# Expert rows sent to their tokens by indirect transfers through DRAM in place of scatter products, in three of four expert groups of one layer

## What is computed

```python
g_idx = top-1 of 4 groups;  e_idx = top-2 of that group's 4 experts
w = pg_top * pe_top / sum(pe_top)
expert = g_idx * 4 + e_idx
gates = sum(one_hot(expert, 16) * w[..., None], axis=1)
for e in range(16):
    he = silu(t @ w1[e]) * (t @ w3[e])        # 1024 -> 512
    out = out + gates[:, e:e + 1] * (he @ w2[e])   # 512 -> 1024
```

## Time and profile before

| | us |
|---|---|
| median of 3 runs | 892.6 (890.75 to 893.31) |
| the profiled execution | 893.93 |
| its span | 892.2 |
| TensorE busy | 830.9 (93%) |
| DVE, ACT, POOL busy | 317.2, 201.9, 151.8 |

### The profile page before, as it was taken

The page is one execution under the profiler, slowest core; times in us unless marked ns, Lnnn a source line. Parts: engine busy times, 40 slices in busy tenths (PEclk is TensorE's granted clock), DMA queues, the critical chain, the costliest instruction groups (busy, mean ns, idle before and its releaser), DMA issues.

```text
span 892.2 us, 12858 instructions
## 1 busy us (share of the span) xinstructions
PE 830.9 (93%) x5263; PEld 459.3 (51%) x5264; DVE 317.2 (36%) x720; ACT 201.9 (23%) x332; POOL 151.8 (17%) x242
## 2 busy tenths in 40 slices
PE   3899989899999999999499999699999899999994
PEld 1367644565465564655456554434444554655651
DVE  1437994551131321411799421621000311311304
ACT  2403330531221311312500110411001211312212
POOL 2418679039200000000133100100000000000000
PEclk9899999999999999999799999889999999999998
DMA  9999999949999999994996882206766299999972
GB/s 329 345 363 387 346 374 324 364 178 423 421 422 421 421 422 423 422 421 170 391 339 235 305 334 98 92 1 237 307 240 251 99 415 421 419 424 421 422 296 72
DMA packets 69185, 285.37 MB, mean 320 GB/s; under 512 B 7260, under 2 KB 8572, under 8 KB 44312
## 3 DMA queue, kind: packets, MB, share of 16 engines
q1 hardware_dynamic: 66208, 277.88, 79.8%
q0 software_dynamic: 2240, 5.24, 1.7%
q10 hardware_dynamic: 696, 1.68, 0.5%
HBM read 279.55 MB, written 5.24 MB: 319 GB/s over the span
## 4 chain that ended last, share of the span: by engine, by line
PE 85%; DVE 8%; DMA 3%; SPq 2%; ACT 1%; issue 1%; DVEq 0%; ACTq 0%
PE PS L1713 22%; PE PS L1732 14%; PE PS L1740 8%; PE PS L1756 7%; PE PS L2019 7%; PE PS L1716 6%; PE PS L1445 4%; PE PS L1671 3%; PE PS L1475 3%; DMA ring<-in_ab_w_in 2%; PE PS L1537 2%; PE PS L2004 2%; PE PS L1554 2%; SPq L379 2%; PE PS L1982 1%
## 5 line engine op out<-in xcount | busy, mean ns | idle before, releaser
L1732 PE MATMUL PS<-ring,work 128*64 128x512 f32 (+1 forms) x512 | 128.4, 595 | 0.0
L1713 PE MATMUL PS<-ring,hT 128*64 128x256 f32 x896 | 107.3, 381 | 0.0
L1713 PE MATMUL PS<-ring,yg 128*64 128x256 f32 x896 | 106.2, 379 | 0.0
L1320 DVE TENSOR_TENSOR work<-work,PS 128x512 f32<-128x512 f32 x32 | 22.0, 688 | 198.7 <-PE PS L1713 150.4
L1713 PEld LDWEIGHTS PS<-ring,hT 128*64 128x64 f32 x896 | 62.5, 137 | 40.5 <-issue 10.3
L1732 PEld LDWEIGHTS PS<-ring,work 128*64 128x64 f32 (+1 forms) x512 | 43.0, 143 | 74.3 <-issue 73.3
L1713 PEld LDWEIGHTS PS<-ring,yg 128*64 128x64 f32 x896 | 64.4, 137 | 32.3
L1740 PE MATMUL PS<-work,xhat 128*128 128x256 f32 (+1 forms) x256 | 68.2, 426 | 7.8 <-issue 7.4
L1324 DVE COPY yg<-PS 128x512 f32<-128x512 f32 x32 | 22.1, 692 | 144.8 <-PE PS L1732 144.8
L1756 PE MATMUL PS<-yg,grow 64*128 64x512 f32 (+1 forms) x256 | 68.0, 606 | 0.0
L1740 PEld LDWEIGHTS PS<-work,xhat 128*128 128x128 f32 x256 | 50.1, 198 | 28.5 <-issue 22.2
(11 more groups left out here) (379 smaller groups left out, 997.9 us busy)
## 6 DMA issues: line engine op xcount, KB each, us to landing
ring<-in_moe_w SPq DMA_DIRECT2D x96, 2048.0 KB, 13.6
ring<-in_ada_w SPq DMA_DIRECT2D x20, 2048.0 KB, 15.8
work<-in_ada_w SPq DMA_DIRECT2D x4, 2048.0 KB, 13.8
ring<-in_s_glu_w SPq DMA_DIRECT2D x4, 2048.0 KB, 17.1
ring<-in_ab_w_in SPq DMA_DIRECT2D x3, 2048.0 KB, 24.1
ring<-in_ab_w_out SPq DMA_DIRECT2D x2, 2048.0 KB, 13.4
ring<-rot_tables SPq DMA_DIRECT2D x2, 2048.0 KB, 10.9
rot_tables<-grow POOLq DMA_DIRECT2D x8, 256.0 KB, 5.6
```

The lines of the kernel that those rows point to most:

```text
L1320: v.tensor_tensor(pairs_out(he[:, e % 2, :]), pairs_out(he[:, e % 2, :]), pairs(bank[1]), ALU.mult).then_inc(S("he_ready"), 1)
L1713: last = mm(dst[64 * u:64 * u + 64, 0:256], hg[k][:, e * P:e * P + 64], w[:, k, 256 * u:256 * u + 256], start=k == 0, stop=k == KD - 1)
L1732: last = mm(dst, left[:, at:at + (64 if narrow else P)], w[:, c4, h * HALF:(h + 1) * HALF], start=c4 == 0, stop=c4 == KF - 1)
```

## The change

In layer 1, groups 0 to 2 (`DIRECT = 3`) no longer use `turn_weights` and `scatter`. A small product, `slot_info`, gives for each slot its destination row number and its gate weight. DVE's `rows_out` multiplies each expert's product by weight and `gfrow` while it takes it from PSUM into `yg`, and GpSimd's `spread` sends the two halves of these rows to the DRAM tensor `y_rows` by indirect transfers, with numbers out of range for unfilled slots. Rows of tokens that the three groups do not serve are cleared by `clear_rows`. SP reads `y_rows` back (`back`, 4 x 512 KB) between the sixth and the seventh weight unit of group 3, and DVE adds it to x in group 3 (`add_back`). With the banks free, hidden products alternate between two bank pairs and the transposes between banks 6 and 7. Group 3 keeps the scatter products and now opens `acc` itself. In both layers the gate arithmetic (`gates`) stands behind the picks. Several semaphores are merged (`table_dve`, `table_act`) without moving work.

```diff
+                if L == 1:
+                    sp_.wait_ge(S("spread_out"), 64 + 32 * EPG * DIRECT)
+                    for w in range(2):
+                        for b in range(NB):
+                            src = y_rows.rearrange("(b p w h) n -> b w p h n", b=NB, w=2, h=2)[b, w]
+                            sp_.dma_start(back[:, w, b, :].rearrange("p (h n) -> p h n", h=2), src).then_inc(
+                                S("rows_back"), 16)
                 for j in range(SLOTS, PER_GROUP):
                     free_slot(n0 + (NG - 1) * PER_GROUP + j)
                     send_expert(L, j, NG - 1)
...
+            def clear_rows():
+                pool.wait_ge(S("gates_ready"), 1)
...
+                ch.link(g.memset(zero_row, 0.0))
+                for b in range(NB):
+                    for w in range(2):
+                        g.indirect_dma_start(y_rows.rearrange("(t h) n -> t (h n)", h=2),
+                                             bass.IndirectOffsetOnAxis(ap=row_no[:, NG - 1, b, w:w + 1], axis=0), zero_row,
+                                             None, bounds_check=2 * T - 1, oob_is_err=False).then_inc(S("spread_out"), 16)
+                pool.wait_ge(S("spread_out"), 64)
+            def spread(i, e):
+                pool.wait_ge(S("y_dve"), PRIMED["y_dve"] + 16 + 4 * i + e + 1)
+                for h in range(2):
+                    g.indirect_dma_start(y_rows[:, :], bass.IndirectOffsetOnAxis(ap=row_no[:, i, e, h:h + 1], axis=0),
+                                         yg[:, e % 2, h * HALF:(h + 1) * HALF], None, bounds_check=4 * T - 1,
+                                         oob_is_err=False).then_inc(S("spread_out"), 16)
+                pool.wait_ge(S("spread_out"), 64 + 32 * (4 * i + e + 1))
+                pool.sem_inc(S("y_gone"), 1)
+
             over_row(1)
+            clear_rows()
+            for i in range(DIRECT):
+                for e in range(EPG):
+                    spread(i, e)
...
+                    def rows_out(e):
+                        dve.wait_ge(S("y_ps"), e0 + e + 1)
+                        dve.wait_ge(S("y_gone"), 1 + e0 - 16 + e)
+                        for h in range(2):
+                            part = slice(h * HALF, (h + 1) * HALF)
+                            last = v.scalar_tensor_tensor(yg[:, e % 2, part], bank[(6 if e == 3 else 4) + h], slot_w[:, e:e + 1],
+                                                          gfrow[:, part], ALU.mult, ALU.mult)
+                        last.then_inc(S("y_dve"), 1)
+                    def add_back(w):
+                        dve.wait_ge(S("rows_back"), 64)
+                        for b in range(NB):
+                            for h in range(2):
+                                part = slice(h * HALF, (h + 1) * HALF)
+                                last = v.tensor_tensor(x[:, b, part], x[:, b, part], back[:, w, b, part], ALU.add)
...
                 slots(krow[:, 0, :])
                 picks(krow[:, 0, :])
                 link(v.tensor_copy(kcur, krow[:, 0, :]))
+                gates()
...
+            def slot_info():
+                for e in range(EPG):
+                    for b in range(NB):
+                        last = mm(bank[7][:, 2 * e:2 * e + 2], pick[:, b, e, :], slot_in[:, b, e, :], start=b == 0,
+                                  stop=b == NB - 1)
+                return last
...
+                    def down_direct(e, narrow):
+                        j = AT[("w2", e)]
+                        loaded(pe, n0 + j, i)
+                        pe.wait_ge(S("heT_ready"), 1 + e0 + e + 1)
+                        if 1 <= e < 3:
+                            pe.wait_ge(S("y_dve"), 1 + e0 + e)
+                        product_down(u3(n0 + j, D), narrow, heTs[e % 2], 6 if e == 3 else 4,
+                                     (lambda: turned_direct(3, narrow)) if e == 2 else None).then_inc(S("y_ps"), 1)
...
                         gather(narrow)
+                        if direct:
+                            slots()
+                            for e in range(EPG):
+                                up(e, narrow)
+                                if e:
+                                    down_direct(e - 1, narrow)
+                            down_direct(EPG - 1, narrow)
+                            return
+                        if L == 1:
+                            for m in range(4):
+                                open_acc(m)
                         up(0, narrow)
```

More of the change, by code:

```diff
@@ L231, in build @@
         strips = pickW[:, :, :, :].rearrange("p b e n -> p (b e n)")[:, 0:T]
+        heTs = [heT, pickW[:, 0].rearrange("p e n -> p (e n)")]
+        first_row = rt[:, 316:318]
+        slot_in = rt[:, 80:96].rearrange("p (b e n) -> p b e n", b=NB, e=EPG)
+        slot_w = rt[:, 96:100]
+        below = before[:, 64:65]
+        miss, none, at_row = rt[:, 240:242], rt[:, 242:246], rt[:, 184:188]
+        y_rows = nc.dram_tensor("y_rows", [4 * T, HALF], F32).ap()
+        back = w3(T0, 2, NB, D)
         krow = rt[:, 248:248 + 9 * (NG + 1)].rearrange("p (g n) -> p g n", n=9)
@@ L461, in _ @@
             g = nc.gpsimd
+            pool.sem_inc(S("y_gone"), PRIMED["y_gone"])
             ch = Chain(pool, S("pool_order"))
@@ L834, in ffn, with group @@
                 pt = lambda m: pickT[:, 2 * m:2 * m + 2, :].rearrange("p e t -> p (e t)")
-                with act.Fori(0, NG) as i:
+                def group(i, direct):
                     gi, e0 = 4 * L + i, 16 * L + 4 * i
@@ L840, in silu, with he_direct @@
                         act.wait_ge(S("a_ps"), e0 + e + 1)
-                        s.activation(pairs_out(he[:, e % 2, :]), pairs(bank[0]), ACT.Silu).then_inc(S("sil_ready"), 1)
+                        s.activation(pairs_out(he[:, e % 2, :]), pairs(bank[e % 2 * 2 if direct else 0]), ACT.Silu).then_inc(
+                            S("sil_ready"), 1)
+                    def he_direct(e):
+                        act.wait_ge(S("heT_ps"), e0 + e + 1)
+                        s.activation(heTs[e % 2], bank[6 + e % 2], ACT.Copy).then_inc(S("heT_ready"), 1)
                     def he_t(e):
@@ L868, in ffn @@
                     y_out(3)
+                with act.Fori(0, NG if L == 0 else DIRECT) as i:
+                    group(i, L == 1)
+                if L == 1:
+                    group(NG - 1, False)
                 act.wait_ge(S("over_known"), L + 1)
@@ L1322, in y_out @@
+                    def add_back(w):
+                        dve.wait_ge(S("rows_back"), 64)
+                        for b in range(NB):
+                            for h in range(2):
+                                part = slice(h * HALF, (h + 1) * HALF)
+                                last = v.tensor_tensor(x[:, b, part], x[:, b, part], back[:, w, b, part], ALU.add)
+                        link(last)
                     def y_out(e):
@@ L1728, in product_down @@
                     steps = [(h, c4) for c4 in range(KF) for h in range(2)]
-                for h, c4 in steps:
+                for n_, (h, c4) in enumerate(steps):
+                    if halfway is not None and n_ == KF:
+                        halfway()
                     at = (c4 % 2) * P + (c4 // 2) * 64 if narrow else c4 * P
@@ L1889, in group, with wide_aside @@
                         spread(3, narrow)
+                    kind = f"{L}d" if direct else f"{L}"
                     is_narrow = pe.value_load(rti[0:1, bass.ds(i + 2, 1)], min_val=0, max_val=1)
                     head = nc.cur_bb
[L1893 to L1894 removed]
+                    nc.br_lt(is_narrow, 1, on_true=f"wide{kind}", on_false=f"narrow{kind}", engines=PE_ONLY)
+                    nc.switch_bb(f"narrow{kind}")
                     group(True)
[L1896 to L1897 removed]
+                    nc.br(f"group_end{kind}", engines=PE_ONLY)
+                    nc.switch_bb(f"group_end{kind}", parent=head)
+                    def wide_aside():
+                        with nc.body(f"wide{kind}", parent=head, valid_engines=PE_ONLY):
+                            group(False)
+                            nc.br(f"group_end{kind}", engines=PE_ONLY)
+                    return wide_aside
+                with pe.Fori(0, NG if L == 0 else DIRECT) as i:
+                    wides = [group_of(i, L == 1)]
+                if L == 1:
+                    wides.append(group_of(NG - 1, False))
                 for _ in range(SLOTS):
@@ L1937, in aside @@
                 def aside():
-                    with nc.body(f"wide{L}", parent=head, valid_engines=PE_ONLY):
-                        group(False)
-                        nc.br(f"group_end{L}", engines=PE_ONLY)
+                    for wide_aside in wides:
+                        wide_aside()
                     with nc.body(f"over{L}", parent=exit_, valid_engines=PE_ONLY):
```

235 lines of the change are left out of this document (167 added, 68 removed).

## The result

The changed kernel takes 878.09 us (median of 4 runs, 876.47 to 879.58), the kernel before 891.93 us in the same comparison. The ratio is 0.9841, 95% interval 0.9817 to 0.9866: 1.6% faster, by 12 to 16 us. The forecast was 12.7 us less, 879.9.

The account below looks back on a forecast made before the run. TensorE and the nearly equal, saturated weight stream bound it; the stream then decides. Last weights 851.6 + 5.0 + 2.6 = 859.2, then 3.5, 3.6 and 1.1: TensorE ends at 867.4 against 880.1; -12.7 from 892.6 gives 879.9 us, range 874 to 889.

Parts of the forecast that it names:

- Part 1: Gate arithmetic behind the picks, both layers: first gather 0.9 us earlier in layer 1, 0.4 us in layer 0.
- taking accumulator openers out of the routing stretch gives nothing: Layer 1's routing stretch: removing openers gains nothing, since TensorE waits for DVE there anyway.
- Part 2: Group 0, TensorE: weight transposes -0.9, scatter products -13.7, slot products +1.8, net -12.8 us.
- Part 3: Layer 1's weight stream starts when group 1's first weights are read, moving from 712.3 to 700.0 us.
- Parts 4 and 5: Groups 1 and 2: TensorE loses 6.7 us each, but the stream decides; read-back adds 4.97 us, scattered rows 2.6.
- Scatters: GpSimd's two transfers take 6 to 12 us an expert, hidden under 15 us (narrow group) or 25 (wide).
- the lock: SBUF: DVE operations in a two-port mode keep GpSimd from writing descriptors; no size given.
- Second rival: GpSimd's scatter sets the pace above 15.2 us an expert; gain gone at 16.8, 918 us at 20; chance 0.10.
- the rule's 15 us: Groups 1 and 2: eight experts each pay the excess of scatter time over 15.2 us.

Follow-up runs that it names:

- The fillers: Changed kernel with four filler products (full 512-column, into banks 4 to 7) where the openers stood in layer 1's routing stretch: 878.89 us, ratio 0.9825.

## Why the prediction was right, and where it was not

The mechanism was right. Group 0 gives its TensorE time in full, groups 1 and 2 give almost none, as the stream of weights takes over, and the read-back lengthens it. The run with one direct group shows the first two: with group 0 alone it is 9.8 us faster than the kernel before (893.35 to 883.55), and its group 0 takes 102.0 us from gather to gather (586.37 to 688.33). The runs without the read-back and with it last show the third.

- *Part 1.* Layer 0's gather comes 3.96 us after the last rank product instead of 4.53, so it gave 0.6 us, forecast 0.4. In layer 1 the step "taking accumulator openers out of the routing stretch gives nothing" was wrong: it costs 1.0 us through the clock, so that the part's 0.9 us came to nothing. The fillers show it, and the two later runs with fillers have 18.4 and 18.5 us.
- *Part 2.* Group 0 without the passage went from 115.1 to 101.8 us, -13.3; forecast -12.8. The slot products took 1.84 us, forecast 1.8.
- *Part 3.* The stream starts at 694.2, not at 700.0. Of the 5.8 us, 2.4 are the idle time after the wide group, which I had carried over unchanged, and 1.7 the cold gather behind it (8.78 against 7.07); the run with the added wait shows what the passage hangs on. The rest is 0.5 us of group 0 and the earlier start of the phase, less the lost part 1. The passage is the larger of the two mechanisms that I missed; it is worth about 4 us.
- *Parts 4 and 5.* The stream lasted 160.6 us, forecast 159.2. The read-back cost its 5 us. The rows of groups 1 and 2 were 0.59 MB, not 1.05, but each MB took 3.6 us of the engines and not 2.5; that makes 2.1 us, and with the fading end 2 to 3 us in the whole time. The forecast of 2.6 is near it by two errors against each other. TensorE waited 9.9 us for weights, forecast six to nine. The forecast's 8.2 us from the last weights to TensorE's end came out as 8.3.
- *Scatters.* One expert's pair took 9.3 us on GpSimd from first issue to the next expert's (732.82 to 742.14), forecast 6 to 12. The Trainium skill (DMA: Bandwidth & Descriptors, Anatomy of one DMA) gives an estimate of 2.6 us for one transfer of 256 KB. Against it stand 7.1 us from the end of the second issue to the next expert's first, for a pair and with the engines full; here the measurement decides. Of the lock that the Trainium skill (SBUF — State Buffer, SBUF: two separate sides) describes I see no cost: 16 issues took 0.968 to 1.037 us each. But only five of them ran beside any DVE instruction, the longest beside the picks (800.68), so these runs hardly test it.
- *Second rival.* It did not come true. At 17.1 us an expert the gain is gone, as its break-even of 16.8 us says, but the rule's 15 us were 19.8; where the loss begins was not tried.

The nearness of 879.9 to the measured 878.09 is partly luck. The passage gave 4.1 us that I had not counted, and group 0 and layer 0 gave 0.7 more than forecast; the lost part 1 took back 0.9 and the longer stream 1.4. So corrected, the sum is 12.7 + 4.1 + 0.7 - 0.9 - 1.4 = 15.2 us. The medians are 13.8 us apart in the first comparison and 15.8 in the second (893.66 and 877.89), so they don't tell the forecast from the corrected sum. The 17.0 us between the two profiled executions hold chance besides.

## What to carry to other kernels

Before work is taken from the busiest engine, ask which transfer is queued next to it: here TensorE and the weight stream differed by 10 us in 300, and of 27 us saved work the kernel kept half. What is moved to the stream should be placed where the stream has no successor (the read-back behind the last weights gave 3 to 4 us, in pieces 6 with the fillers). And the last wait before a jump to distant code decides whether the pause after it is seen: keep queued products behind it.

## What was not expected of the hardware

- The passage from the wide to the narrow code takes TensorE 7.7 to 8.6 us from its last wait, against at most 2.8 us between narrow groups; queued products hide it, and one wait of 1.4 us at the wrong place cost 10 to 12 us.
- Products that nobody reads were worth 1.0 us of a stretch: after 3.5 us of idle time the granted clock was 0.50, and the small rank products took 2.3 us instead of 1.3.
- Indirect transfers of 0.59 MB among 58 MB came with a stream whose load faded out over some 3 us, where it had ended within 1 to 2 us; why was not shown.
